# Column-tiled rotary-key and index-key projections, and latent key heads made in pairs, in a two-block float32 kernel

## The reference, cut to what matters

```python
hp = h @ w_in                            # 1024 -> 256 q | 128 kv | 32 rope | conv | fourier | gating | gates
c_q  = rmsnorm(hp[:, 0:256]);   q = c_q @ w_uq            # 4 heads x (64 + 32)
c_kv = rmsnorm(hp[:, 256:384]); kv = c_kv @ w_ukv         # 4 heads x (64 key + 64 value)
k = concat([kv_keys_of_head, rope2d(hp[:, 384:416])])     # the 32 rotary columns are shared by all heads
```

```python
iq, ik, iw = h @ w_in2[...]              # 8 index heads x 64, one index key x 64, 8 weights
score = sum_h iw[h] * relu(iq[h] @ ik.T) # picks the 256 keys of each query
```

## Time and profile before

| | |
|---|---|
| median of three runs | 3547.58 us (3544.61 to 3548.47) |
| profiled execution | 3546.45 us, span 3544.5 us |
| PE busy | 3395.6 us, 96% of the span |
| DVE busy | 1714.0 us, 48% |
| ACT busy | 991.4 us, 28% |
| DMA | 163.73 MB, mean 46 GB/s |

### The profile page before, as it was taken

How to read it: one execution, slowest core, us unless ns; L and a number is a source line. 1 busy time by engine, 2 the same in 40 slices (tenths; PEclk the granted TensorE clock), 3 DMA queues, 4 the chain that set the end, 5 groups by cost and what they waited for, 6 DMA issues and landing times.

```text
span 3544.5 us, 31399 instructions
## 1 busy us (share of the span) xinstructions
PE 3395.6 (96%) x12290; PEld 1795.0 (51%) x12290; DVE 1714.0 (48%) x3094; ACT 991.4 (28%) x2079; POOL 200.1 (6%) x203
## 2 busy tenths in 40 slices
PE   7999999999989999999999899899999999999997
PEld 3556555565446544544565565574444444444443
DVE  2056282143146281451355655474345656555556
ACT  4244211102244201021477854631121000000001
POOL 0000000020000000100000000000110001112020
PEclk9999999999999999999999999899999999999999
DMA  5100122130100001101001011211101111111112
GB/s 210 57 7 13 56 74 80 45 119 24 36 12 13 23 33 45 45 33 54 31 36 36 18 33 33 72 60 47 36 12 36 48 36 48 37 53 42 42 42 71
DMA packets 52209, 163.73 MB, mean 46 GB/s; under 512 B 5552, under 2 KB 9904, under 8 KB 51389
## 3 DMA queue, kind: packets, MB, share of 16 engines
q1 hardware_dynamic: 47194, 145.82, 11.9%
q10 hardware_dynamic: 4868, 15.91, 1.3%
HBM read 157.46 MB, written 11.32 MB: 48 GB/s over the span
## 4 chain that ended last, share of the span: by engine, by line
PE 86%; DVE 7%; ACT 4%; issue 1%; SPq 1%; DMA 0%; POOL 0%; DVEq 0%; ACTq 0%; POOLq 0%
PE ps L605 27%; PE ps L635 15%; PE ps L1285 14%; PE ps L1047 5%; PE ps L763 4%; PE ps L1058 2%; PE ps L786 2%; PE ps L942 2%; PE ps L775 2%; PE ps L1070 2%; ACT sb L1821 1%; PE ps L1125 1%; PE ps L1136 1%; DVE sb L2081 1%; PE ps L1032 1%
## 5 line engine op out<-in xcount | busy, mean ns | idle before, releaser
L605 PE MATMUL ps<-sb 128*128 128x512 f32 (+1 forms) x2448 | 963.5, 554 | 14.0 <-ACT sb L1624 6.7
L1344 ACT ACTIVATE sb<-ps 128x512 f32<-128x512 f32 (+10 forms) x729 | 363.2, 514 | 1597.0 <-PE ps L605 465.9
L605 PEld LDWEIGHTS ps<-sb 128*128 128x128 f32 x2448 | 466.5, 191 | 505.0 <-issue 479.6
L635 PE MATMUL ps<-sb 128*128 128x512 f32 x1232 | 532.7, 593 | 2.5 <-ACT sb L1344 1.9
L1285 PE MATMUL ps<-sb 128*128 128x512 f32 x1232 | 530.5, 592 | 3.7 <-DVE sb L2710 3.7
L1285 PEld LDWEIGHTS ps<-sb 128*128 128x128 f32 x1232 | 233.8, 190 | 299.4 <-issue 292.3
L635 PEld LDWEIGHTS ps<-sb 128*128 128x128 f32 x1232 | 233.7, 190 | 297.5 <-issue 290.4
L1047 PE MATMUL ps<-sb 128*128 128x512 f32 x512 | 231.3, 599 | 0.0
L763 PE MATMUL ps<-sb 96*128 96x512 f32 (+1 forms) x400 | 157.4, 529 | 5.2 <-ACT sb L1533 4.5
L2217 DVE SCALAR_TENSOR_TENSOR sb<-sb 128x1310 f32<-128x1310 f32 (+1 forms) x120 | 161.7, 1426 | 0.0
L1821 ACT ACTIVATE sb<-sb 128x384 int8<-128x384 f32 (+4 forms) x160 | 152.2, 953 | 2.3 <-DVE sb L2376 0.7
(11 more groups left out here) (264 smaller groups left out, 3392.7 us busy)
## 6 DMA issues: line engine op xcount, KB each, us to landing
sb<-in_w_in SPq DMA_DIRECT2D x73, 512.0 KB, 3.3
sb<-in_w_ada SPq DMA_DIRECT2D x48, 512.0 KB, 4.4
sb<-in_w_up SPq DMA_DIRECT2D x44, 512.0 KB, 3.3
sb<-in_w_down SPq DMA_DIRECT2D x40, 256.0 KB, 2.8
sb<-in_w_out SPq DMA_DIRECT2D x16, 512.0 KB, 3.6
sb<-in_w_mkv SPq DMA_DIRECT2D x16, 512.0 KB, 3.3
rows_dram<-vec_dram ACTq DMA_DIRECT2D x1, 6906.0 KB
sb<-rows_dram ACTq DMA_DIRECT2D x6, 1024.0 KB, 5.2
```

The costliest lines, as they stand in the source:

```text
L605: ins = mm(ps[:, 0:tn], w[:, k, :], src(k, t0, tn), start=(k == 0), stop=(k == nk - 1))
L635: ins = mm(ps[:, 0:512], stationary(k), moving(k), start=(first and k == 0), stop=(k == h - 1), skip_group_check=not first)
L1344: return act(out, in_, func, scale=scale)
```

## The change

**The rotary key.** Its weights become a tile of their own, `w_rope`: 1024 x 32 (as eight pieces of 128 x 32), and a folding matrix of 128 x 128 that holds 64 zero columns, the identity of 32 four times on the partitions, and the same with swapped columns. The 24 products have 32 output features and go to four groups of partitions in turn. ACT copies the partial sums of each chunk to `rope_part`, and `fold_rope` makes the 128 rows by one product a chunk. These three folds take the first places of `query_key_sum`: two after the first chunk of g0, the third after the second chunk, ahead of the first norm sum. The tile is released by the third fold. The context part is now copied by DVE.

**The index key.** The 1024 inputs are cut in two halves; each half makes 64 features in its own group of 64 partitions, and a fold adds the halves and writes them twice. The folding matrix lies in the tile `w_iw`, which is now released by the second fold. The order becomes iq2, ik halves, iq3, iw fold, ik folds.

**The latent key heads.** One product makes the 128 features of two heads, and ACT evicts its halves with two copies. `head_jobs` has no jobs for heads 1 and 3 any more, and the pairs 5 of both layers have no job at all.

```diff
-    first = [("q", 0, 0), ("k", 0, 0), ("k", 0, 1), ("k", 0, 2), ("q", 1, 0), ("k", 1, 0), ("k", 1, 1), ("k", 1, 2),
-             ("q", 0, 1), ("q", 1, 1)]
+    first = [("q", 0, 0), ("k", 0, 0), ("q", 1, 0), ("k", 0, 1), ("q", 0, 1), ("k", 0, 2), ("q", 1, 1)]
...
-                ps = psum.take(e, (l, "kh", h, c, "ps"), (l, "kh", h, c, "ev"), 1, pool)
-                mm(ps[0:64, 0:tn], wk[:, h * 64:(h + 1) * 64], mkv[:, t0:t0 + tn], start=True, stop=True).then_inc(*e.step((l, "kh", h, c)))
+                ps = psum.take(e, (l, "kh", h, c, "ps"), [(l, "kh", h + j, c, "ev") for j in range(2)], 1, pool)
+                mm(ps[:, 0:tn], wk[:, h * 64:(h + 2) * 64], mkv[:, t0:t0 + tn], start=True, stop=True).then_inc(*e.step((l, "kh", h, c)))
...
-            w_in(3, "rope", CHUNKS, lambda c: (l, "rope", "ev", c) if c < 2 else (l, "kr", 2, 1))
+            rope_w = ring.take(e, f"w_rope{l}", 0, 384, ((l, "rope"), 2, "mm"))
+            rope_quarters, rope_fold = rope_w[:, 0:256].rearrange("p (k m) -> p k m", m=32), rope_w[:, 256:384]
+            for c, (t0, tn) in enumerate(CHUNKS):
+                ps = psum.take(e, (l, "rope part ps", c), (l, "rope part", c))
+                for k in range(KD):
+                    e.wait_ge(*at((l, "h", c, k)))
+                    q = 32 * (k % 4)
+                    ins = mm(ps[q:q + 32, 0:tn], rope_quarters[:, k, :], H[:, k, t0:t0 + tn], start=(k < 4), stop=(k >= 4))
+                ins.then_inc(*e.step((l, "rope part mm", c)))
...
+            def fold_rope(c):
+
+                tn = CHUNKS[c][1]
+                ps = psum.take(e, ((l, "rope"), c), (l, "rope", "ev", c) if c < 2 else (l, "kr", 2, 1), 1, "mla turns")
+                e.wait_ge(*at((l, "rope part", c)))
+                mm(ps[:, 0:tn], rope_fold, rope_part[:, CHUNKS[c][0]:CHUNKS[c][0] + tn], start=True, stop=True).then_inc(
+                    *e.step(((l, "rope"), c, "mm")))
+
             def query_key_sum():
 
-                if waiting:
+                if len(to_fold) == 3:
+                    fold_rope(to_fold.pop(0))
+                    fold_rope(to_fold.pop(0))
+                elif waiting:
+                    if to_fold:
+                        fold_rope(to_fold.pop(0))
                     name, c, nk = waiting.pop(0)
                     norm_sums((l, name), (c,), nk, "mla turns")
...
-        w = ring.take(e, "w_iw", 0, 256, ("iw part mm", 1)).rearrange("p (k m) -> p k m", m=32)
+        iw_tile = ring.take(e, "w_iw", 0, 384, ("ik", 1, "mm"))
+        w, ik_fold = iw_tile[:, 0:256].rearrange("p (k m) -> p k m", m=32), iw_tile[:, 256:384]
...
+            for k in range(4):
+                for a in range(2):
+                    ins = mm(ps[64 * a:64 * a + 64, 0:512], w[:, 4 * a + k, 64 * a:64 * a + 64],
+                             H2[:, 4 * a + k, 512 * c:512 * c + 512], start=(k == 0), stop=(k == 3))
...
+        for c in range(2):
+            e.wait_ge(*at(("ik part", c)))
+            ps = psum.take(e, ("ik", c), ("ik", "ev", c))
+            mm(ps[:, 0:512], ik_fold, ir[:, 1, 512 * c:512 * c + 512], start=True, stop=True).then_inc(*e.step(("ik", c, "mm")))
```

More of the change, by code:

```diff
@@ L839, in w_in @@
                     ada(*tile)
-                if key in ("rope", "g7"):
+                if key == "g7":
                     turn_rows()
@@ L853, in first_block @@
             w_in(2, "kv", CHUNKS)
-            w_in(3, "rope", CHUNKS, lambda c: (l, "rope", "ev", c) if c < 2 else (l, "kr", 2, 1))
-            waiting = [("qn", c, 2) for c in oc] + [("kn", c, 1) for c in range(3)]
-            def query_key_sum():
-                if waiting:
+            rope_w = ring.take(e, f"w_rope{l}", 0, 384, ((l, "rope"), 2, "mm"))
[7 more added lines that the diff above has]
+                ins.then_inc(*e.step((l, "rope part mm", c)))
+            for tile in later_ada(l).get("rope", ()):
+                ada(*tile)
+            turn_rows()
+            to_fold = [0, 1, 2]
+            waiting = [("qn", c, 2) for c in oc] + [("kn", c, 1) for c in range(3)]
+            def fold_rope(c):
[4 more added lines that the diff above has]
+                    *e.step(((l, "rope"), c, "mm")))
+            def query_key_sum():
+                if len(to_fold) == 3:
[4 more added lines that the diff above has]
+                        fold_rope(to_fold.pop(0))
                     name, c, nk = waiting.pop(0)
                     norm_sums((l, name), (c,), nk, "mla turns")
-            w_in(10, "g0", pool="mla scores", behind=query_key_sum)
-            w_in(11, "g1", pool="mla scores", behind=query_key_sum)
+            w_in(9, "g0", pool="mla scores", behind=query_key_sum)
+            w_in(10, "g1", pool="mla scores", behind=query_key_sum)
             while waiting:
@@ L1011, in tensor_program @@
             ins.then_inc(*e.step(("iw part mm", c)))
-        for i in range(2, 4):
-            w_in2(i, f"iq{i}")
-        w_in2(4, "ik")
+        w_in2(2, "iq2")
+        w = ring.take(e, "w_in2", 4, 1024, ("ik part mm", 1)).rearrange("p (k m) -> p k m", m=P)
+        for c in range(2):
+            ps = psum.take(e, ("ik part ps", c), ("ik part", c))
+            for k in range(4):
+                for a in range(2):
+                    ins = mm(ps[64 * a:64 * a + 64, 0:512], w[:, 4 * a + k, 64 * a:64 * a + 64],
+                             H2[:, 4 * a + k, 512 * c:512 * c + 512], start=(k == 0), stop=(k == 3))
+            ins.then_inc(*e.step(("ik part mm", c)))
+        w_in2(3, "iq3")
         ps = psum.take(e, "iw ps", "iw")
@@ L1506, in project @@
                 e.wait_ge(*at((l, "kh", h, c)))
-                copy(kh[0:64, h, t0:t0 + tn], psum.at((l, "kh", h, c, "ps"))[0:64, 0:tn]).then_inc(*e.step((l, "kh", h, c, "ev")))
+                for j in range(2):
+                    copy(kh[0:64, h + j, t0:t0 + tn], psum.at((l, "kh", h, c, "ps"))[64 * j:64 * j + 64, 0:tn]).then_inc(
+                        *e.step((l, "kh", h + j, c, "ev")))
         def turned(l, u, t, g):
@@ L1577, in first_block @@
             later("kv")
-            e.wait_ge(*at(((l, "rope"), 2, "mm")))
-            for j in range(2):
-                copy(kh[64:96, j, N:T], psum.at(((l, "rope"), 2))[64:96, 0:L]).then_inc(*e.step((l, "kr", 2, j)))
+            for c, (t0, tn) in enumerate(CHUNKS):
+                e.wait_ge(*at((l, "rope part mm", c)))
+                copy(rope_part[:, t0:t0 + tn], psum.at((l, "rope part ps", c))[:, 0:tn]).then_inc(*e.step((l, "rope part", c)))
             later("rope")
@@ L1687, in scalar_program @@
                 *e.step(("iw part", c)))
-        for i in range(2, 4):
-            for c in range(2):
-                evict_index(f"iq{i}", iq[:, i, 512 * c:512 * c + 512], c)
+        for c in range(2):
+            evict_index("iq2", iq[:, 2, 512 * c:512 * c + 512], c)
+        for c in range(2):
+            e.wait_ge(*at(("ik part mm", c)))
+            copy(ir[:, 1, 512 * c:512 * c + 512], psum.at(("ik part ps", c))[:, 0:512]).then_inc(*e.step(("ik part", c)))
+        for c in range(2):
+            evict_index("iq3", iq[:, 3, 512 * c:512 * c + 512], c)
         for c in range(2):
@@ L2166, in first_block @@
                 rope_read[0] = (l, "kr", c, 1)
+            e.wait_ge(*at(((l, "rope"), 2, "mm")))
+            for j in range(2):
+                v.tensor_copy(kh[64:96, j, N:T], psum.at(((l, "rope"), 2))[64:96, 0:L]).then_inc(*e.step((l, "kr", 2, j)))
             scale_rows((l, "qn"), oc, 2, lambda k, t0, tn: mq[:, k, t0:t0 + tn], lambda k, t0, tn: mq[:, k, t0:t0 + tn],
```

27 lines of the change are left out of this document (15 added, 12 removed).

## The result

The changed kernel takes 3522.89 us (median of four runs, 3520.07 to 3523.49) against 3547.51 (3544.61 to 3548.47): a ratio of 0.9935 with an interval of 0.992 to 0.995. The forecast was 3517, the range 3509 to 3529; the measured time lies in the range, and 0.9 us beyond the 3512 to 3522 that the forecast gave itself before a rival begins. The profiled execution took 3520.07 us, span 3518.2, which is 26.3 under the span before; the sum had said 30.9.

A forecast was written before the change was run, and what follows sets the result against it. PE was taken to bound the kernel, with 86% of the last-ending chain. Gains of 38.2 us less losses of 7.3 give 30.9 off 3546.45, 3515.5; with 1.1 to the median 3516.6, said as 3517, range 3509 to 3529.

The forecast's parts named there:

- Products: PE's cheaper products: rotary key saves 21.0 us, index key 5.3, key heads 8.8; quarters 4.7 a layer, halves 7.0.
- the iw row: Profile row of the index weights: 16 products of 32 features took 3.6 us, 0.225 each; used to price the rotary quarters.
- some 36: Sign that would show the forecast: PE's busy time down by some 36 us; under 30 would make it wrong.
- Norm chain: Ahead of the value products: norm sums one place later, added waits of 2.0 us in layer 0, 0.7 in layer 1, 2.7 together.
- Index scores: Two gaps around the first index scores, 1.4 us for ACT's copy and 1.1 for the k0 load; 3.0 us taken.
- more is given back: Rival: new gaps lower the clock or the k0 load is held up; four places at up to 2.9 us, 3528; chance 0.14.
- First scores of layer 1: Layer 1's first score tiles wait for a bank holding the last query projection: 1.6 us lost.
- which DVE reads twice after it ends: Step behind the 1.6 us: DVE reads the last query projection's bank twice, 2 x 0.69 + 0.2.
- The clock: Slower products behind new gaps under a lowered granted clock: taken as 0, with 0 to 3 us at the index scores.
- The pairs: Attention pairs: pair 5 without a job frees a wait in each layer, 1.7 us gained; no new waits expected.
- one such wait a layer goes: 1.7 us: Jobs in the attention pairs wait 0.83 us for a DVE copy's bank; pair 5's job goes, 1.7 us gained.
- the attention slows: Rival: changed bank order makes each of 36 pairs wait; 0.83 us each leaves nothing, 1.9 each gives 3585; chance 0.02.

The follow-up runs named there:

- one_column_group: Changed kernel with all eight products of a rotary chunk in the same group of 32 columns: 3544.85 us, 1.0001 of before.
- changed_again: The changed kernel itself, unedited, measured again beside the next experiments: 3519.12 us, 0.9928 of the kernel before.
- banks_of_layer_1: Changed kernel with layer 1's bank rotations started so that no score tile stands on the last query projection's bank: 3512.03 us, 0.9903 of before.
- rope_only: Changed kernel with only the rotary quarters kept, index key and key heads taken back: 3532.16 us, 0.9968 of before.
- folds_around_sums: Changed kernel with the first rotary fold behind the first norm sum, the second ahead of and third behind the second sum: 3512.57 us, 0.9907 of before.

## Why the prediction was right, and what it mis-sized

- **Products.** 4.7 us a layer for the quarters, 7.1 for the halves, folds without a gap, 34.1 us off PE's busy time for 35.1: right, with the iw row as the price. With the slow products taken out PE's work fell by 37 to 38, 2 to 3 more than said, most of it with the heads ("some 36" under what would show it was a little more than its own sum). The Trainium skill (TensorE: Matmul & The Clock Gate, Part 3, Measured speedup vs the span model), by the estimate scaled from it, would have made the quarters about 1 us a layer dearer; the trace, with 4.48 and 4.50 us, goes by the row. one_column_group shows that the overlap is the cause for the quarters.
- **Norm chain.** Said 2.7. From the last kn sum that runs without a wait to the first query product, with the extra sum (0.86) taken off, layer 0 needs 1.5 us more than before (157.45 to 172.46, against 169.27 to 181.92) and layer 1 0.7 more. 2.2, so right. In changed_again the same two are 1.4 more and 1.0 less, since the value products of layer 1 ran faster there.
- **Index scores.** Said 3.0 for two gaps; they are 3.4, with 1.7 more in slow products. From iw's start to the second score pair the changed kernel needs 0.55 us more than before (51.68 us, 1571.01 to 1622.69, against 51.13, 1600.89 to 1652.02), where the forecast had a net gain of 2.3. So in this stretch the index key gave back all that it saved. The landing of 4.3 us instead of 3.3 is what the second half of the rival "more is given back" spoke of; as a cause it is not shown.
- **First scores of layer 1: mis-sized.** Said 2 x 0.69 + 0.2 = 1.6 us; it was 3.05. The step "which DVE reads twice after it ends" took DVE to be free when the last query ended. It was not: each rotation waits for GpSimd's sum of the one before, 2.92 us a head, and with the key products gone from between them the queries come faster than that. The wait fell on this tile only because of the bank rotation; banks_of_layer_1 took it away with another start of the rotation.
- **The clock: the term that failed.** It stood at 0 (0 to 3). Slow products behind the new or neighbouring gaps cost, by the trace, 1.7 us at the index scores, and in layer 1 4.08 + 7.88 us for nine products that need 2.31 + 4.46: 5.2, where before's 6.23 in the earlier trace rows had 1.7. The value products changed by -0.5 in layer 0 and +0.5 in layer 1. That is some 5 us given back at the gaps, and 3.1 more in the stretch from 1931 us, which the change doesn't touch. Elsewhere the changed kernel lost less to the clock than before did, so that over the whole execution "slow" rose by 4.0 us. In changed_again, the same kernel, it fell by 8.3. By the medians the clock took some 4 to 6 us, an estimate: 24.6 to 26.6 us gained, where work and idle time say 30.0 to 30.3. The rival "more is given back" had the right mechanism, and at 3528 too high a price: its four places at 2.9 us each were 11.6.
- **The sum without the clock** came out at 30.0 to 30.3 us for 30.9. That is luck in part: work fell by 2 to 3 us more than said, and idle time rose by 7.1 to 7.9 us where the sum had 4.2.
- **The pairs: mis-sized.** The forecast took "one such wait a layer goes: 1.7 us" as gained and named new waits in the pairs as a sign of being wrong. Layer 1 has none. Layer 0 has one of 0.40 us in pair 5, and one that grew from 0.46 to 0.83, so of the 1.7 us about 0.9 came. The rival "the attention slows" needed 0.86 us in each of 36 pairs and did not come.

Left open: why the clock falls in one run and not in another after waits of the same length. The profile shows the same waits and both outcomes. So it is not shown either how much of the 4 to 6 us the change itself causes: the slow products behind its gaps are in both profiled executions of the changed kernel, the total is not.

## What to carry to other kernels

When PE's work gets cheaper, look at what it covered: the slot that its last product releases, the bank that the rotation hands out next, and the pace of the DVE-GpSimd chain behind it. Small folds belong where other products cover both their copies and the next load; moving them, with the new bank start, took 11 us of idle time away (156.8 to 145.4), where the whole index key was worth 3. Price a gap with the slow products that follow it. Before believing a difference of a few microseconds, part each profiled execution into work, slow and idle. Span times granted clock is a quicker look, but it was off by up to 5 us here (rope_only, 21.4 for 16.6), and it hid the gain of folds_around_sums.

## What the runs showed of the hardware

- Products with 32 output features that went to four groups of 32 partitions in turn cost 0.225 us each, a full one 0.88 (3.9 times), those with 64 features in two groups half as much as a full one (16 products of 512 columns in 7.09 us), and those with 32 features in one group alone as much as full ones (24 products in about 17.2 us, against 17.45).
- The mean granted clock of one kernel varied from 0.982 to 0.988 from run to run, 17 us in 3520. In two executions with nearly the same work (3319.3 and 3320.3 us) and idle time (156.8 and 156.1), the lowered clock cost 42.1 and 29.8 us.
- Filling a 4.76 us wait with products brought the ones after it back to full clock (6.95 to 4.55 us), and brought the kernel nothing, with the waits elsewhere left (3520.44 us) or mostly gone (3493.53). A second filling, behind a shorter wait at the low clock, took 5.09 us for three products and made its layer no shorter.
